# A fused three-layer kernel: the seams ahead of two MLPs done one token block at a time

## The reference

```python
for i in range(2):
    pre = rms_norm(h, norm_g[i, 0])
    mix = s5_mixer(pre, ...) if i == 0 else dsa_mixer(pre, ...)      # SSM, then top-k attention
    h = h + rms_norm(mix, norm_g[i, 1])
    ff = sq_relu_mlp(rms_norm(h, norm_g[i, 2]), mlp_w1[i], mlp_w2[i])
    h = h + rms_norm(ff, norm_g[i, 3])

def rms_norm(x, g):   # x * rsqrt(mean(x * x) + 1e-6) * g
def sq_relu_mlp(h, w1, w2):
    a = relu(h @ w1)          # 1024 -> 4096
    return (a * a) @ w2       # 4096 -> 1024
```

## Time and profile before

| | us |
|---|---|
| three runs | 1341.96, 1341.98, 1348.33 (median 1341.98) |
| profiled execution, own time | 1347.69 |
| its span, first to last instruction | 1345.8 |
| TensorE busy | 1286.8 (96%) |
| DVE busy | 1024.0 (76%) |
| ACT busy | 670.9 (50%) |
| POOL busy | 419.1 (31%) |

### The profile page before, as it was taken

How to read it: one execution, slowest core, us unless ns; L and a number is a source line. 1 busy time by engine, 2 the same in 40 slices (tenths; PEclk the granted TensorE clock), 3 DMA queues, 4 the chain that set the end, 5 groups by cost and what they waited for, 6 DMA issues and landing times.

```text
span 1345.8 us, 20924 instructions
## 1 busy us (share of the span) xinstructions
PE 1286.8 (96%) x7700; PEld 1096.1 (81%) x7700; DVE 1024.0 (76%) x1483; ACT 670.9 (50%) x1124; POOL 419.1 (31%) x215
## 2 busy tenths in 40 slices
PE   6998999998889999999999999999999989999998
PEld 5876888877667788887788888899999947899998
DVE  7986777776764777776687545499999985699997
ACT  5765444444454544444545444355554523455553
POOL 5014444433202544443435212210000002345553
PEclk9999999999889999999999899999999989999999
DMA  7045665645213455553657423354454324366663
GB/s 212 32 130 168 188 188 189 197 121 188 63 63 126 156 188 187 187 187 98 204 168 219 117 90 94 94 157 127 154 156 127 125 62 141 91 191 187 188 187 110
DMA packets 166364, 197.12 MB, mean 146 GB/s; under 512 B 9982, under 2 KB 131326, under 8 KB 166270
## 3 DMA queue, kind: packets, MB, share of 16 engines
q1 hardware_dynamic: 164939, 191.54, 46.1%
q10 hardware_dynamic: 1362, 4.74, 1.0%
HBM read 195.20 MB, written 1.05 MB: 146 GB/s over the span
## 4 chain that ended last, share of the span: by engine, by line
PE 68%; DVE 21%; ACT 4%; issue 3%; DMA 2%; POOL 1%; DVEq 0%; SPq 0%; ACTq 0%
PE acc L685 20%; PE wk L637 9%; PE wk L601 6%; PE wk L603 6%; PE wk L602 6%; PE wk L639 5%; DVE LO L1948 4%; DVE arena L2517 2%; PE wk L1163 1%; PE acc L601 1%; PE acc L898 1%; PE acc L1189 1%; PE acc L602 1%; PE acc L603 1%; DVE LO L462 1%
## 5 line engine op out<-in xcount | busy, mean ns | idle before, releaser
L462 POOL TENSOR_TENSOR LO<-raw,HI 128x1024 fp32r<-128x1024 f32 (+1 forms) x162 | 387.5, 2398 | 847.6 <-ACT HI L1408 770.1
L1408 ACT ACTIVATE HI<-raw 128x1024 fp32r<-128x1024 f32 (+3 forms) x382 | 365.2, 996 | 118.9 <-DMA raw<-in_w_in 34.5
L462 DVE TENSOR_TENSOR LO<-raw,HI 128x1024 fp32r<-128x1024 f32 (+1 forms) x160 | 263.3, 1648 | 97.8 <-ACT HI L1408 97.5
L601 PE MATMUL wk<-X,HI 128*128 128x256 f32 x784 | 224.7, 287 | 3.2 <-DVE X L1981 1.2
L602 PE MATMUL wk<-X,HI 128*128 128x256 f32 x784 | 222.0, 283 | 0.0
L603 PE MATMUL wk<-X,LO 128*128 128x256 f32 x784 | 222.0, 283 | 0.0
L637 PE MATMUL wk<-X,HI 128*128 128x512 f32 x512 | 183.7, 401 | 2.5 <-DVE X L1981 2.5
L601 PEld LDWEIGHTS wk<-X,HI 128*128 128x128 f32 x784 | 150.3, 192 | 6.8 <-issue 2.8
L602 PEld LDWEIGHTS wk<-X,HI 128*128 128x128 f32 x784 | 150.4, 192 | 0.8
L603 PEld LDWEIGHTS wk<-X,LO 128*128 128x128 f32 x784 | 150.4, 192 | 0.0
L639 PE MATMUL wk<-X,LO 128*128 128x256 f32 x512 | 144.3, 282 | 0.0
(11 more groups left out here) (387 smaller groups left out, 2196.9 us busy)
## 6 DMA issues: line engine op xcount, KB each, us to landing
raw<-in_mlp_w SPq DMA_DIRECT2D x128, 512.0 KB, 3.8
raw<-in_w_in SPq DMA_DIRECT2D x100, 512.0 KB, 4.2
raw<-in_w_up SPq DMA_DIRECT2D x44, 512.0 KB, 3.9
raw<-in_w_down SPq DMA_DIRECT2D x44, 256.0 KB, 3.1
raw<-in_att_w_in SPq DMA_DIRECT2D x16, 512.0 KB, 3.9
raw<-in_w_ssd_proj SPq DMA_DIRECT2D x16, 512.0 KB, 3.7
raw<-in_att_w_out SPq DMA_DIRECT2D x8, 512.0 KB, 4.2
raw<-in_w_out SPq DMA_DIRECT2D x8, 512.0 KB, 4.2
```

Of the source, the lines that this page charges most:

```text
L462: tensor_tensor(LO[:, s, cs], raw[:, s % 2, "ab".index(part), 0:m], HI[:, s, cs].bitcast(F32), ALU.subtract).then_inc(S(f"lo_{part}"), 1)
L601: mm(o, lh, rh, start=start, stop=False, skip_group_check=skip)
L1408: A(HI[:, s, j * m:(j + 1) * m], raw[:, s % 2, j, 0:m], ACT.Copy).then_inc(S(f"hi_{part}"), 1)
```

## The change

- TensorE: mlp no longer calls norm_transpose for all four quarters with 20 and 2 dummies. It issues 12 dummies and the transposes of block 0, the first up chunk for block 0 (ch_block), 4 dummies and the transposes of block 1, the chunk for block 1, then clear_acc. ch_block does a pair of 256 and 128 columns for each j and k, 16 pairs a block, 32 in all.
- DVE and ACT: post, pre and xT are replaced by by_block in both seams. BY_BLOCK is range(1, 9).
- POOL: row_rstd(1) and row_rstd(2) become row_rstd(1, 2), and the same for 5 and 6.
- DVE: the parameter instructions move from ahead of the first seam into the first MLP, behind hidden_low(0, 0).

```diff
-        BY_BLOCK = (3, 4, 7, 8)
+        BY_BLOCK = range(1, 9)
...
-            row_rstd(1)
-            row_rstd(2)
+            row_rstd(1, 2)
...
-            row_rstd(5)
-            row_rstd(6)
+            row_rstd(5, 6)
...
+            def ch_block(s, bank, tb, norm):
+
+                ts = slice(tb * P, (tb + 1) * P)
+                for j in range(2):
+                    o = wk[:, bank + j, :].rearrange("p (r t) -> p r t", r=2)
+                    for k in range(KD):
+                        w = k * 256 + j * P
+                        if j == 0:
+                            xT_wait(norm, tb, k)
+                        mm(o[:, :, ts], HI[:, s, w:w + P], X2[:, k, :, ts], start=k == 0, stop=False, skip_group_check=True)
+                        last = mm(o[:, 0, ts], LO[:, s, w:w + P], XH[:, k, ts], start=False, stop=k == KD - 1,
+                                  skip_group_check=True)
+                return last
...
             def mlp(layer):                                   # TensorE
-                norm_transpose(1 + 2 * layer, 20, 2)
-                base = layer * MC
+                base, n = layer * MC, 1 + 2 * layer
+                norm_transpose(n, 12, 0, (0, 1))
+                s = arrived()
+                for tb in range(TB):
+                    if tb == 1:
+                        norm_transpose(n, 4, 0, (2, 3))
+                    last = ch_block(s, 0, tb, n)
+                used(last)
+                clear_acc()
...
-                mlp_up(0, 0)
-                clear_acc()
                 turn(0)
...
-            post(1, 4)                                        # ACT
+            by_block(0, 1, 4, 1)
             def mlp(layer, first):
-                pre(2 * layer)
-                xT_high(1 + 2 * layer)
...
-            post(3, P_ATT + 12)
+            by_block(2, 3, P_ATT + 12, 3)
             mlp(1, P_ATT + 13)
...
-            TS(cols[:, 2, R_QG:R_QG + 1], ...)                # DVE: the parameter instructions,
...
-            link(last)
             lo_to(6)
-            post(0, 1)
+            by_block(0, 1, 1)
+            def block2_params():                              # the same instructions, in here
...
             def mlp(layer, first):
-                pre(1 + 2 * layer, 2 + 4 * layer)
-                xT_low(1 + 2 * layer)
...
                 hidden_low(0, 0)
+                if layer == 0:
+                    block2_params()
...
-            post(2, 5)
+            by_block(2, 5, 3)
             mlp(1, P_ATT + 13)
```

More of the change, by code:

```diff
@@ L627, in back_turned, with ch_wide @@
                 return last
-            def ch_wide(s, bank, norm=None):
+            def ch_block(s, bank, tb, norm):
[10 more added lines that the diff above has]
+                return last
+            def ch_wide(s, bank):
                 for j in range(2):
@@ L634, in ch_wide @@
                         w = k * 256 + j * P
-                        if norm is not None and j == 0:
-                            xT_wait(norm, 1, k)
                         mm(o, HI[:, s, w:w + P], X2[:, k, :, :].rearrange("p r t -> p (r t)"), start=k == 0, stop=False,
@@ L865, in mlp_up @@
                     s = arrived()
-                    used(ch_wide(s, 2 * par, norm=1 + 2 * layer if isinstance(c, int) and c == 0 else None))
+                    used(ch_wide(s, 2 * par))
                 def mlp_down(c, par, end=False):
@@ L1432, in post_block @@
                     squares(acc, tb, n, sem, count)
-            def post(n, last_piece):
-                for tb in range(TB):
-                    post_block(n, last_piece, tb)
             def pre_block(j, tb):
@@ L1997, in residual @@
                         .then_inc(S("h_ready"), 1)
[L1999 to L2003, removed]
             def by_block(j, e, n):
@@ L2199, in _ @@
             V.tensor_copy(neg_bf[:, :], cst[:, C_NEGT:C_NEGT + P])
[L2201 to L2216, removed]
@@ L2217, in _ @@
-            link(last)
-            lo_to(6)
-            post(0, 1)
+            lo_to(6)
+            by_block(0, 1, 1)
+            def block2_params():
+                TS(cols[:, 2, R_QG:R_QG + 1], cols[:, 2, R_QG:R_QG + 1], -HD ** -0.5, None, ALU.mult)
+                cw = cols[:, 1, :].rearrange("p (k t) -> p k t", k=4)
+                for j in range(2):
+                    TS(gpall[:, :, G_WX + j:G_WX + 8:2], cw[:, :, j:16:2].rearrange("p k g -> p g k"), 0.5, None, ALU.mult)
+                    TS(gpall[:, :, G_BX + j], cols[:, 2, R_CB + j:R_CB + 16:2], 0.5, None, ALU.mult)
+                    V.tensor_copy(gpall[:, :, G_NG + j], cols[:, 2, R_SN + j:R_SN + 16:2])
+                    V.tensor_copy(gpall[:, :, G_D + j], pairb[:, 16 + j:32:2])
+                TS(gpall[:, :, G_WB:G_WB + 4], cw[:, :, 16:24].rearrange("p k g -> p g k"), 0.5, None, ALU.mult)
+                TS(gpall[:, :, G_WC:G_WC + 4], cw[:, :, 24:32].rearrange("p k g -> p g k"), 0.5, None, ALU.mult)
+                TS(gpall[:, :, G_BB], cols[:, 2, R_CB + 16:R_CB + 24], 0.5, None, ALU.mult)
+                TS(gpall[:, :, G_BC], cols[:, 2, R_CB + 24:R_CB + 32], 0.5, None, ALU.mult)
+                for j, f in enumerate((0.5, 1.0)):
+                    for k in range(3):
+                        blk, at = (3, k * 44) if k < 2 else (4, 0)
+                        TS(fpall[:, :, 4 * j + k], cols[:, blk, at + FC * j:at + FC * (j + 1)], f, None, ALU.mult)
+                    last = TS(fpall[:, :, 4 * j + 3], cols[:, 2, R_FB + FC * j:R_FB + FC * (j + 1)], f, None, ALU.mult)
+                link(last)
```

## The result

| | before | changed |
|---|---|---|
| median, 20 runs each | 1345.48 us (1340.93 to 1352.42) | 1349.26 us (1343.97 to 1354.67) |
| ratio to before | | 1.0029, 95% interval 1.0016 to 1.0041 |
| profiled execution, own time | 1347.69 | 1353.39 |
| its span | 1345.8 | 1351.5 |

The change makes the kernel slower by 0.3% (3.9 us by the ratio), clear of noise but under the 0.5% that the forecast called a change. The forecast was 1344.1 on a median of 1341.98 from three runs, +2.1 us; 1349.26 lies inside 1339 to 1349.5, near its edge. Part of that distance is the median of before itself, which 20 runs put 3.5 us higher. The range that the forecast's own sum gave, 1341.5 to 1345.5, does not reach 1349.26.

A forecast was written before the change was run, and what follows sets the result against it. TensorE, busy 96% of the span, bounds the kernel, so only the seams count: A (ahead of the first MLP) +1.1, B (ahead of the second) +1.0, the rest 0, giving 1344.1 us on a 1341.98 median; range 1339 to 1349.5.

The forecast's parts named there:

- the upper place: Rival: the runs settle in the upper of their two places, 6.3 us above, at 1350 us; chance 0.09.
- The chain of DVE, ACT and POOL: In both seams: pre-norm 0 comes 3.32 us behind residual 0, and block 1's pre-norm 3.32 behind residual 1.
- The half: First up chunk for one block: 0.207 us a pair, 3.3 us a half, bounds 2.8 to 3.75.
- The clock in A: Seam ahead of the first MLP: clock likely halved for 3.4 us from block 0's half, making the seam +1.1 us.
- The clock in B: Seam ahead of the second MLP: a fall less likely; +1.0 us with the clock held, +2.4 with a fall.
- the gate closes on block 0's half in both seams: Rival: clock lowered during block 0's half in both seams, +4.5 us, 1346.5 us; chance 0.17.
- The parameters: Parameter instructions moved into the first MLP: cost 0, covered by 3.2 us of slack and DVE's idle time; gain 0.
- the forecast's own signs of being wrong: Clear_acc of the second MLP's seam before 453.7, a half under 2.8 us, or TensorE idling inside the MLPs.
- The first down chunk: Behind the seam ahead of the second MLP: a new TensorE wait of nothing to 0.1 us, taken as nothing.
- No overlap: Rival: TensorE holds block 1 back, both halves run behind the late chain, +7.3 us, 1349.3 us; chance 0.04.

The follow-up runs named there:

- after_filled: The changed kernel with more dummy matmuls in the gaps of both seams: 1347.94 us, 1.0024 of the kernel before.
- halves_only: The kernel before, its order kept on every engine, with only the first up chunk of each MLP in two halves: 0.9978 of the kernel before.
- seam_b_only: The kernel before with only the seam ahead of the second MLP going block by block with halves: 1340.97 us, one execution.
- params_back: The changed kernel with the parameter instructions back ahead of the first seam: 1348.24 us, 1.0028 of the kernel before.
- params_only: The kernel before with only the parameter instructions moved into the first MLP: 1.0006 of the kernel before.

## Why the prediction was right, and where it was off

- **The number.** That 1349.26 lies in the stated range is in part luck. The range went up to 1349.5 only to meet the rival of the upper place, which did not happen. As a difference the forecast was better: +2.1, with bounds from 0 to +3.5, for +3.9 (2.2 to 5.5).
- **The chain of DVE, ACT and POOL.** Right to 0.1 us: 3.32, 3.86 and 3.31 where 3.32, 3.81 and 3.32 stood. The step that decided the sign is that residual 1 comes later than before, because pre-norm 0, scaled 1 and xT_low stand ahead of it: in the old order it started 2.7 behind residual 0, now 7.2. Together with the halves this costs +1.8 and +1.7 at full clock (after_filled). The halves alone cost 0.4 and 0.7 (halves_only), so they are not the whole of it; the new order with a whole chunk at full clock was not seen.
- **The half.** The term of 0.207 us a pair was too small: 0.234, at the upper bound of 0.235. A pair of 256 and 128 columns took what two 256-column matmuls do by the forecast's own estimate (2 x 0.117, a third of 0.352 each), so halving the columns of the second won nothing against it; the row taken as nearest (32-column matmuls, 0.09 each) was not near. This is most of why B at full clock came to +1.7 for the forecast +1.0: 0.45 in the second half, and the first, at 3.75, made the transposes 0.1 late (seam_b_only) where they were to be just free.
- **The clock in A.** That it would fall was right. Mis-sized was the stretch: 3.4 us were taken from the earlier trace rows, 5.5 were measured, so block 0's half took 6.3 for 5.0 (about 1.0 of it by the stretch and 0.3 by the pairs). With 0.45 more in the second half, A came to +2.9 for +1.1.
- **The clock in B.** The likeliest case had it hold; in the profiled execution it fell and block 0's half took 5.3 us (447.42 to 452.71), in params_back and seam_b_only with the same seam it held. So the profiled execution is the rival "the gate closes on block 0's half in both seams", which had 0.17 and a sum of +4.5; the two seams measured +6.1. Over 20 runs the ratio lies between the forecast and that rival, +3.9.
- **The parameters.** Forecast 0, measured +1.1 in the changed kernel. The step that failed: the slack of 3.2 us was read from the old seam, though the forecast itself had LO and HL shift behind the new one. They shift further than TensorE does: in the changed kernel HL(0) started at 129.53 for a first down at 130.57, in params_only at 123.39 for 126.75. Two edits that are each free spend the same slack: 1.6 us go to the seam and 1.8 to the move when each is alone, 4.1 when both are there. One of the forecast's own signs of being wrong, TensorE idle inside an MLP, came true. That the move wins nothing ahead of seam A was right (params_only).
- **The first down chunk** needed no wait, as forecast: its records show no idle before it.
- **The upper place.** With 20 runs there are no two places, only a spread of 11 us; that rival rested on three runs.
- **No overlap** is out: block 0's half does run while block 1's norm is made.

What stays open is how the +3.9 divides. The order with its halves is +3.5 at full clock (after_filled against old seams without a fall). The parameters are +1.1, in both traces that have them with the new seam A. The falls are in before as well; where one shows, it costs 1.4 (old A), 2.5 to 3.0 (new A) or 1.6 (new B). Together that is more than the runs show, 3.9 with an interval of 2.2 to 5.5, so something that these traces don't locate goes the other way.

The granted clock of every execution helps a little. Its mean is 0.9892 over the changed kernel's 20 and 0.9906 over 34 executions of the kernel before that were taken beside params_back. The 0.0014 between them are 1.9 us of 1347, an estimate, and uncertain by as much, of the most that the clock can account for. after_filled has 0.9920, a higher clock than before, and is still 1.0024 of it: a cost is left that is not the clock's.

## What to carry to other kernels

Interleaving by block puts the first block's later steps ahead of the second block's earlier ones on every serial engine. It costs where both blocks are there nearly together and the work pulled forward is short: here 4.5 us of delay on DVE for half a chunk. That it pays where the second block's input comes late is my guess; no run here tests it. Before a split, ask what a piece costs on TensorE when its columns halve but its weight loads don't: here 7.5 us for 5.6. Before an edit spends slack on an engine, ask what other edits spend of the same slack: the moved parameters were free alone, and cost 1.1 us with the new seam. And a real instruction that has no inputs to wait for, like clear_acc, is a better filler of a gap than a dummy: 0.66 and 1.09 us a seam in the traces.

## What the runs showed of the hardware

- Granted clock: the half that began at 111.18 on a fallen clock ran 5.5 us at 0.50, though TensorE was busy in all of them; before, 3.4 us. The same seam with the same dummies kept its clock in one execution and lost it in another (old A at 23.29 and 21.91, new B at 25.27 and 23.70). At 0.50 a pair took 0.43 us (111.53 to 111.96 from one L637 to the next), at 1.00 0.23.
- A DVE tensor_scalar of 22 columns takes 0.18 us alone; the group of three that started at 131.51, as POOL's LO ran from 131.48 for 2.39, took 2.56. In params_only it was 2.59 beside a LO of 2.40 from 125.34. In the kernel before another one of the same block was hit, 32 columns from 96.11 in 2.33, ending at 98.44 as POOL's LO did at 98.39. So such small instructions were cheap in number and dear in place. HL took 0.69 by itself and 2.89 beside POOL's LO (133.39, POOL from 133.24 for 2.50).
